# Ordering TensorE's blocks by pairs of units in the first attention of a two-network kernel

## What is computed

```python
def global_gqa(...):                      # 8 heads, 2 key/value heads
    k_all = jnp.concatenate([k_ctx, k_lat], 1)      # 512 keys
    p = jax.nn.softmax(gqa_scores(q, k_all), axis=-1)
    return gqa_out(p, v_all)
    ...
    p = jax.nn.softmax(gqa_scores(qc, k_ctx), axis=-1)   # context queries: 256 keys

def neighbourhood_attention(...):         # 8 heads
    s_nb = jnp.einsum(...) + bias[None]             # scores of the latent keys, with a bias by position
    s_ctx = jnp.einsum('brwhd,bthd->bhrwt', qblk, k_ctx)
    p = jax.nn.softmax(jnp.concatenate([s_nb, s_ctx], -1), axis=-1)
    return (... p_nb, vn) + (... p_ctx, v_ctx)

y_lat = jnp.concatenate([ya, yb], -1) @ w_out
```

## Time and profile before

| | |
|---|---|
| Runs, median (lowest to highest) | 1577.86 us (1577.64 to 1578.1) |
| The profiled execution | 1578.89 us |
| Its span, first to last instruction | 1577.4 us |
| TensorE busy | 1546.5 us, 98% |
| VectorE, ScalarE, GpSimd busy | 1065.2, 880.5, 341.6 us |
| First attention on TensorE | about 134 to 224.29 us |

### The profile page before, as it was taken

The page is one execution under the profiler, slowest core; times in us unless marked ns, Lnnn a source line. Parts: engine busy times, 40 slices in busy tenths (PEclk is TensorE's granted clock), DMA queues, the critical chain, the costliest instruction groups (busy, mean ns, idle before and its releaser), DMA issues.

```text
span 1577.4 us, 25520 instructions
## 1 busy us (share of the span) xinstructions
PE 1546.5 (98%) x9936; PEld 1320.7 (84%) x9936; DVE 1065.2 (68%) x1982; ACT 880.5 (56%) x1735; POOL 341.6 (22%) x341
## 2 busy tenths in 40 slices
PE   7999999999999999999999999999999999999998
PEld 4788778988887888887999988888888898788886
DVE  4743766666444525788787777767888667779874
ACT  2423873666652423568555555755766557567662
POOL 0201420355540000112011103242221014412210
PEclk9999999999999999999999999999999999999999
DMA  9766023345667224011555463424555543335551
GB/s 365 300 241 241 19 84 134 120 182 205 234 230 256 83 104 160 14 69 68 187 188 224 171 223 111 147 94 164 187 187 188 199 152 145 135 135 187 187 203 78
DMA packets 46952, 260.35 MB, mean 165 GB/s; under 512 B 11889, under 2 KB 13169, under 8 KB 18161
## 3 DMA queue, kind: packets, MB, share of 16 engines
q1 hardware_dynamic: 43952, 252.78, 43.9%
q0 software_dynamic: 1296, 4.72, 0.8%
q10 hardware_dynamic: 1584, 1.23, 0.2%
HBM read 257.64 MB, written 1.07 MB: 164 GB/s over the span
## 4 chain that ended last, share of the span: by engine, by line
PE 90%; DVE 4%; ACT 3%; DMA 1%; issue 1%; POOL 0%; another core or an unknown queue 0%; DVEq 0%; ACTq 0%
PE ps L512 22%; PE ps L514 21%; PE ps L513 21%; PE ps L764 8%; PE ps L765 5%; PE ps L667 2%; PE ps L689 2%; PE ps L676 2%; PE ps L528 2%; PE ps L1164 1%; PE ps L766 1%; DMA raw<-in_ada 1%; PE ps L575 1%; ACT arena L1825 1%; ACT arena L1500 1%
## 5 line engine op out<-in xcount | busy, mean ns | idle before, releaser
L1925 DVE TENSOR_TENSOR wl<-raw,wh 128x1024 fp32r<-128x1024 f32 (+2 forms) x308 | 362.2, 1217 | 249.5 <-ACT wh L1435 248.2
L1435 ACT CAST wh<-raw 128x1024 fp32r<-128x1024 f32 (+1 forms) x318 | 313.5, 1036 | 328.4 <-PE ps L514 294.2
L512 PE MATMUL ps<-xx,wh 128*128 128x256 f32 (+1 forms) x1006 | 328.4, 326 | 0.1
L514 PE MATMUL ps<-xx,wl 128*128 128x256 f32 (+1 forms) x1006 | 325.5, 324 | 0.0
L513 PE MATMUL ps<-xx,wh 128*128 128x256 f32 (+1 forms) x1006 | 325.4, 323 | 0.0
L512 PE MATMUL ps<-wh,xx 128*128 128x512 f32 (+2 forms) x780 | 286.0, 367 | 5.0 <-DVE wl L1925 1.9
L514 PE MATMUL ps<-wh,xx 128*128 128x512 f32 (+2 forms) x780 | 281.2, 360 | 0.0
L513 PE MATMUL ps<-wl,xx 128*128 128x512 f32 (+2 forms) x780 | 281.0, 360 | 0.0
L2296 DVE SCALAR_TENSOR_TENSOR arena<-ps,pv,arena 128x254 f32<-128x254 f32 (+2 forms) x352 | 193.0, 548 | 28.7 <-ACT arena L1635 19.3
L512 PEld LDWEIGHTS ps<-xx,wh 128*128 128x128 f32 x1006 | 191.2, 190 | 20.6 <-issue 4.0
L514 PEld LDWEIGHTS ps<-xx,wl 128*128 128x128 f32 x1006 | 191.2, 190 | 15.2
(11 more groups left out here) (242 smaller groups left out, 2232.2 us busy)
## 6 DMA issues: line engine op xcount, KB each, us to landing
raw<-in_ada SPq DMA_DIRECT2D x46, 1024.0 KB, 4.9
raw<-in_up SPq DMA_DIRECT2D x44, 1024.0 KB, 4.9
raw<-in_fin SPq DMA_DIRECT2D x44, 1024.0 KB, 4.8
raw<-in_down SPq DMA_DIRECT2D x22, 1024.0 KB, 4.8
raw<-in_fout SPq DMA_DIRECT2D x22, 1024.0 KB, 4.9
raw<-in_win SPq DMA_DIRECT2D x12, 1024.0 KB, 4.9
raw<-in_ev_w_in SPq DMA_DIRECT2D x9, 1024.0 KB, 7.0
raw<-in_wout SPq DMA_DIRECT2D x8, 1024.0 KB, 4.9
```

Source lines behind the costliest of these rows:

```text
L512: e.matmul(out, A[0], B[0], start=first, stop=False)
L514: return e.matmul(out, A[1], B[0], start=False, stop=last)
L1435: e.copy(hi_of(j)[:, a:b], raw_of(j)[:, a:b]).then_inc(*S.hi.up((j, half)))
L1925: e.tensor_tensor(lo_of(j)[:, a:b], raw_of(j)[:, a:b], hi_of(j)[:, a:b].bitcast(F), ALU.subtract).then_inc(*S.lo.up((j, half)))
```

## The change

For the key "ev" alone TensorE walks the units in pairs: the scores of both, the transposes of the unit two behind the first, the values of the units four and three behind, and then the transposes of the unit one behind the first. No other engine's program changes, and the second layer's attention keeps its loop.

```diff
+            if key == "ev":
+                for i in range(0, A.n + 4, 2):
+                    for unit in (i, i + 1):
+                        if unit < A.n:
+                            scores(unit)
+                            fill(unit)
+                    if 0 <= i - 2 < A.n:
+                        transposes(i - 2)
+                    for unit in (i - 4, i - 3):
+                        if unit >= 0:
+                            values(unit)
+                    if 0 <= i - 1 < A.n:
+                        transposes(i - 1)
+                return
             for i in range(A.n + A.lag + 1):
                 if i < A.n:
                     scores(i)
```

## The result

| | before | after |
|---|---|---|
| Median (lowest to highest), 7 runs each | 1578.33 us (1577.64 to 1580.18) | 1584.04 us (1582.07 to 1587.3) |
| The profiled execution | 1578.89 us | 1582.07 us |
| Its span | 1577.4 us | 1580.8 us |
| Output rows start on TensorE | 224.29 us | 227.54 us |

After over before is 1.0035, 95% interval 1.0026 to 1.0045: the change makes the kernel slower by some 5.5 us (5.7 by the medians). The prediction had the sign and the places of the waits right, and the size too small: 1581.5 us with an upper end of 1583.5, against 1584.04. The profiled execution of the new kernel is one of the two fastest of its seven, so its profile, 3.2 us over that of before, shows the order's own cost and not all of the difference.

What follows compares the result with a forecast made beforehand. TensorE, busy 98%, bounds the kernel through when it leaves the first attention. Work to 221.1 us plus 7.1 of waits gave 228.2, 3.9 later; the middle of 3.3 and 3.9 on 1577.86 gave 1581.5 us, range 1578.8 to 1583.5.

Steps and rivals of the forecast that it cites:

- the walk: Going through four engine queues with measured durations: attention ends at 224.34 us before, 228.2 after; without the stall 223.8 and 227.1.
- S(13): TensorE's scores of unit 13: forecast wait of 0.61 us, together with the transposes of unit 11.
- T(14): TensorE's transposes of unit 14: forecast wait 0.75 us, for ScalarE's copy of unit 13 behind two casts.
- T(22): TensorE's transposes of unit 22: forecast wait 1.81 us, for the copy of unit 21 behind unit 23's exponentials; work 0.88.
- The path of a plain pair: From a unit's scores through maximum, exponentials and copy to the pair's second transposes: 4.54 us against 4.85 of lead.
- rival B: TensorE's waits on copies don't come up; it leaves the attention at 221.1 us, 3.2 earlier: 1574.7 us; chance 0.08.
- rival C: ScalarE's unchanged total work sets the attention's end: 225.2 us, 0.9 later than now, 1578.8 us; chance 0.15.
- The second cost: ScalarE gets a pair's scores close together, then idles until the next pair's first maximum: 0.95 us at unit 12.
- I take no extra price for the new joints: TensorE's transposes behind values: no extra cost; a pair of units costs 5.88 us instead of 6.23.
- I take that stall at the same time: ScalarE's 2.44 us stall of unknown releaser, held to 166.60 us: transposes of unit 5 start at 167.33 in both kernels.
- so I price no clock loss: TensorE's granted clock stayed at 1.00 through the wait before unit 5's transposes, so no loss was counted.
- rival D: One further wait feeds back, as when the unknown stall meets no lead: 2.4 us later again, 1583.9 us; chance 0.09.

Runs made afterwards that it cites:

- e3: Changed kernel with the second values and second transposes of each pair in each other's places: 1592.37 us, 1.0082 of the kernel before.
- e8: Scores and transposes alternate at the old distance of three units, only values go by twos: 1582.81 us, 1.0032 of the kernel before.
- e1: The kernel before run again, unchanged: 1579.45 us, 1.0000 of the kernel before.
- e13: Kernel before with gate-row writes moved out of the attention and GpSimd's masks of tables 0 to 3 at steps 8 and 10: 1577.67 us.
- e2: The changed kernel run again, unchanged: 1585.02 us, 1.0032 of the kernel before.
- e7: Kernel before with the four early weight casts behind units 5, 7, 9, 11 instead of 15 to 21: 1579.71 us, 1.0002 of before.
- e14: Changed kernel with gate-row writes moved out of the attention and GpSimd's masks of tables 0 to 3 at steps 8 and 10: 1582.08 us.
- e15: Kernel before with a hand-written mixed order, early casts behind units 5 to 11, gate-row writes out of the attention, masks at 8 and 10: 1576.12 us.
- e5: Kernel before with the gate-row writes issued behind the last bias tables, at 195 to 197 us instead of 144: 1584.95 us.
- e6: Changed kernel with the gate-row writes issued behind the last bias tables, at 195 to 197 us instead of 144: 1587.70 us.
- e4: Changed kernel with the four early weight casts behind units 5, 7, 9, 11 instead of 15 to 21: 1583.95 us, 1.0031 of before.
- e9: Kernel before with gate-row writes moved out of the attention, ahead of the `ev_w_out` loads and into the feed-forward network: 1584.26 us.

## Why the prediction was right, and where it was wrong

**Right: what bounds the kernel.** The end of the attention moved, and the rest shifted with it: 1353.1 to 1353.4 us behind it in all kernels.

**Right: the waits, by place and size.** Counted as the walk counts them, by the distance of starts beyond the work, the changed kernel's profile has against the walk:

| block | walked | measured | from |
|---|---|---|---|
| T(7) | 0.15 | 0.16 | 172.19 - 170.13 - 1.90 |
| S(13), T(11) | 0.61 | 0.77 | 0.31 and 0.46 |
| T(13) | 0.15 | 0.15 | 190.83 - 188.78 - 1.90 |
| T(14) | 0.75 | 0.77 | 194.57 - 191.87 - 1.93 |
| S(19), T(16), T(17) | 1.70 | 1.62 | 201.67 - 198.58 - 1.93, and 0.46 |
| T(18) | 0.28 | 0.28 | 208.33 - 206.12 - 1.93 |
| S(23), T(20) | 1.19 | 1.11 | 215.38 - 212.34 - 1.93 |
| T(22) | 1.81 | 1.82 | 221.20 - 218.35 - 1.03 |
| T(23) | 0.44 | 0.46 | 224.60 - 222.24 - 1.90 |
| sum | 7.1 | 7.1 | |

T(14), the copy behind two casts, and T(22), the copy behind four exponentials, were worked out to 0.02 us; single terms are up to 0.16 off, and that the sum agrees to 0.1 is in part luck. The path of a plain pair was put at 4.54 us against a lead of 4.85: e3 took 1.02 us of that lead away, and every pair waited. So rival B (no waits) and rival C (total work alone) both fall: B by 1.74 us ahead of T(22), C by e3. The second cost that the prediction names shows too: the waits of ScalarE for values, of which e8 has the most.

**Too small: the work of the new order, 0.5 us.** "I take no extra price for the new joints" was a step that failed. From T(5) to the output rows there are 61.40 us (166.14 to 227.54); less 7.14 of waits that is 54.26, against 53.8 in the walk. T(22) cost 1.04 us and not 0.88: 0.16. Two values blocks ahead of transposes cost 1.93 us where nothing waits (176.18 to 178.11), and 1.90 was taken from the pair with the output rows behind it: 0.03 four times. The other transposes cost 0.01 to 0.03 more than 1.02 or 1.03 (the second of a pair 1.05, 178.11 to 179.16), some 0.2 in all. Up to T(5) the walk had 0.2 too much, so the new attention came out 0.3 us over it (92.25 against 92.0). The old one came out 0.35 under it (88.33 in e1 and e13, against 88.7 without the stall). Together that is why the order costs 3.95 us in the attention where the walk had 3.3.

**Wrong: what the stall does.** "I take that stall at the same time", the same in both kernels, then "so I price no clock loss", and for the median "the middle of 3.3 and 3.9". The clock is the step that failed: it was put at nothing, and it measured 1.6 us in e2's profile, where the stall is. The walk with the stall has T(5) 32.2 us behind the first scores (135.12 to 167.33) and then 60.9 us to the output rows, 93.1 in all. e2 has 32.6 (134.90 to 167.51) and then 62.95, 95.56 in all. Of the 2.5 us more, 0.4 are the stall's own, 0.5 the work of the paragraph above, and 1.6 the clock at 0.51 and 0.64 behind a wait of 2.15. So the walk let the stall cost 1.1 us in the new order (228.2 - 227.1), and in e2 it costs 3.3 (95.56 against 92.25); in the kernel before it costs 0.83 (89.16 against 88.33), where S(9) is still to do when it comes.

That is one execution of each, and the stall differs from one to the next: in e7 it cost the old order 4.8 us, clock loss included, and e1's ten executions of the kernel before reach 1582.46. What the medians say is less. The new order costs 5.7 us with the writes in the attention (1584.04 - 1578.33; again 5.6, e2 against e1) and 4.4 with them elsewhere (e14 against e13): 1.2 to 1.3 us of the difference go with the writes. That the shorter lead is why the stall costs the new order more is argued from e2 against before, and not shown.

This is rival D, which stood at 0.09: one more wait where the unknown stall meets no lead. In its number it comes close (1583.9 against 1584.04), but by luck: it has 2.4 us more in every execution, where the runs show 1.2 to 1.3 in the median, and the rest of the way is made up by other errors. I had read the earlier trace rows as a piece of the kernel and the earlier trace rows as proof that the clock holds; one execution with 0.77 us of wait can't show what 2.15 does.

**The sum again.** 1577.86 was the median of three runs; in the seven runs beside after it was 1578.33: 0.5. The order itself costs 4.4 us where the walk without the stall had 3.3: 1.1. The stall adds 1.3, where the middle of 3.3 and 3.9 had allowed it 0.3: 1.0. That is 2.6 us above 1581.5, 1584.1 us against the measured 1584.04. The sum closes because the 1.3 is what the difference of 5.7 leaves over the 4.4; it is no check of its own. The upper end of the range, 1583.5, was 5.7 later on 1577.86, built from wrong joints alone. The measured difference is those 5.7, but joints that save nothing aren't how it came about, and the 0.5 us of the median of before put it outside. The range had no term for the stall's scatter, although D was at hand; with 2.4 us for it, it would have held the result.

On the Trainium skill (TensorEngine Tiling, Key Properties), the drain at a change of tiling mode: the traces agree that a joint has a price, 5.93 us for a pair instead of 6.23 with two joints fewer (that it is the drain, they don't show), and e15 shows that it can be had, 0.8 us of it, if no transposes lose their lead. Its warning that the copies out of PSUM may become the bound (PSUM Bottleneck) came true in a way: TensorE waits for copies, though ScalarE is busy 18.36 us of 20 at the most; what makes them late is the order in which they stand behind exponentials.

## What to carry to other kernels

When blocks of an engine are grouped to save joints, write down for each block that needs another engine's answer how much work stands ahead of it (the lead) and how long the answer's path is, with every instruction that stands in the queue ahead of it; the shortest lead decides, and 0.3 us of joint saved a pair is soon lost to one unit kind whose path is 0.2 us too long. Group only where the lead allows, as e15 does. And take a stall of unknown cause in the one profiled execution as something that will fall differently on the next: price it once at the old lead and once at the new, and look at the granted clock behind waits of that length before putting its loss at nothing.

## What the runs showed of the hardware

- **Engines stall after many small writes.** Four DMAs of 1,024 elements of 4 bytes each are followed, some 10 to 20 us after they are issued, by waits of 2 to 5 us of ScalarE and VectorE, in the trace of before for signals of TensorE's blocks that had ended 2.0 and 2.5 us earlier. In e5 and e7 TensorE itself stands still inside a block (1.74 and 1.94 us). Moved by 50 us, the stall moves by 50 us (e5); with the writes elsewhere, 11 runs lie within 0.75 us (e13) where before 31 spread over 2.0, though e14's nine still spread over 3.7. It is not in every execution (none in e1 and after). Why is not shown.
- **The granted clock falls after a wait, in some cases.** It stood at about 0.5 after TensorE's waits of 2.15 us (e2), 2.47 (e6), 2.6 (e4) and 4.6 (e9), for some 3 to 4 us, and stayed at 1.00 after 1.74 (after) and, in e3, after 2.05. But the length of one wait isn't all: in e8 it fell behind two waits of 0.91 and 0.98 with 1.1 us of scores between them. What decides isn't settled by these runs. The Trainium skill (TensorE: Matmul & The Clock Gate, What's actually happening) says that the clock depends on TensorE's recent activity; these traces agree, in that each fall comes behind waits.
- **One queue's edit showed up on another's.** Writing the gate rows earlier on SyncE put 4.6 us of wait on TensorE, through a table, GpSimd's masks and its normalisation (e9), and two changed step numbers took it away again (e13).
